# Even mixer: rotated queries and keys turned by way of HBM and VectorE's 32x32 blocks, and one weight remainder computed behind the score maxima

## The chip, the cores and the metric

The kernel runs on one core of one Trainium2 chip. The metric is the device time of one execution in microseconds (us); lower is better.

## What is computed

The program is two transformer blocks in float32 on one sequence of 256 tokens by 1024 features. The first block (two hybrid layers and a norm) is not touched. The second has an even mixer and an odd mixer; the change lies in the even mixer. Cut to what matters:

```python
def even_mixer(h, w_in, pool_w, pool_scale, w_out):
    z = h @ w_in                                   # 256 x 3072, six groups of 512
    q, k, v, ga, pu, gb = split(z)                 # 512 columns each
    q = rope_partial(q.reshape(b, s, 4, 128))      # first 32 of each head's 128 features are rotated
    k = rope_partial(k.reshape(b, s, 4, 128))
    att = moba_attention(q, k, v).reshape(b, s, A) * silu(ga)   # here: causal attention over 256 tokens
    pool = multiscale_pool(pu, pool_w, pool_scale) * silu(gb)   # means over windows of 2, 4, 8, 16 tokens
    return concatenate([att, pool]) @ w_out
```

The scores contract over a head's 128 features, so queries and keys must stand with features on the partitions, while the product h @ w_in of these groups leaves them with tokens on the partitions. Each must be turned.

## The kernel before

The engines are programmed by hand: each block (`sync`, `tensor`, `scalar`, `vector`, `gpsimd`) is a list of instructions in the order in which its engine runs them, and semaphores are the only tie between them. Every matrix product is split into a high and a low part. A weight piece is 128 partitions x 4 x 512 floats (1 MB). SP loads it (L683) into one of four raw slots as soon as VectorE (DVE) has finished with the slot's last piece; ScalarE (ACT) rounds it to `w_hi` (L1518, `split`), DVE computes the remainder `w_lo` = raw - `w_hi` (L1911, `split`), and TensorE (PE) makes three products of them. `step(p)` splits piece p + 2, on ACT as on DVE. `piece_used` counts the pieces that PE is done with; three pieces fit in `w_hi` and `w_lo`.

The even mixer's twelve weight pieces are called E+0 to E+11 here (E is `E_PIECE`). Two pieces make one group of 512 columns: queries (E+0, E+1), keys (E+2, E+3), values (E+4, E+5), the pool input (E+6, E+7), the gate of the pool (E+8, E+9) and the gate of the attention (E+10, E+11). The first three groups come out with tokens on the partitions (`mixer_first`, `tokens_out`), the last three with features on them (`features_out`).

On PE the order is: queries, keys, values; then 16 transposes of 128x128 (L1308) that put queries and keys into four PSUM banks, `TURN`, after `rope2_done` has reached 4; then the pool input; the scores (L1314, L1315), which wait for `q2T_ready` and `k2T_ready`; the gate of the pool; one of four column blocks of the attention's gate, the transposes of the probabilities (L1323) and the pool's product (L1328), which waits for `pool_mean`; and the rest.

ACT evacuates the query and key groups as they are to `zq` and `zk` (`evacuate`, L1530). DVE rotates them there (`rotate_second`, L2289 to L2295). After the transposes ACT copies the turned queries to `q2T` (L1765), DVE the turned keys to `k2T` (L2313). DVE then splits E+9 and E+10, and only then runs through the four heads' scores: scale and mask, two maxima and their negation (L2318 to L2323). ACT's exponentials (L1774) follow each head's maxima, then the Silu table and the gate's evacuation; DVE normalises (L2326, L2329) and splits E+11 and E+12. GpSimd (POOL) computes the window means in `pool_means` (L2572 to L2584) once the pool input has been evacuated and the turned queries and keys have left the area that it writes.

The first block already moves other tensors through HBM: SP stores them to a bounce tensor (`store_rows`, L688) and fetches them back in 32-feature blocks with four DMAs, one per block of partitions (`fetch_blocks`, L694), and DVE turns each 32x32 block in place (`turn_blocks`, L2036). All DMAs are issued by SP, in the order of its list. The names `arena` and `raw` in the profile are areas that many tensors share; `q2T`, `k2T`, `zq`, `zk` and the pool's tensors all read `arena` there.

Of the kernel before, what the change touches and what calls it, by code (L numbers as in the profile page):

```python
# [6 lines left out]
F32 = mybir.dt.float32  # L7
# [5 lines left out]
P = 128  # L13
# [154 lines left out]
def build_program(nc, ins, consts, where, out):  # L168
    ctx = ExitStack()
    with ctx:  # L170
# [147 lines left out]
        q2T = area(11264, ATT2_HEADS, SEQ)  # L318
        k2T = area(12288, ATT2_HEADS, SEQ)
        probs2 = area(13312, ATT2_HEADS, 384)  # L320
        probs2T = area(11264, ATT2_HEADS, 384)
# [143 lines left out]
        rope2_done = sem("rope2_done")  # L465
        qk2_turned = sem("qk2_turned")
        q2T_ready = sem("q2T_ready")
# [170 lines left out]
        def _(sp):  # L638
# [84 lines left out]
            for l in range(DEPTH):  # L723
# [15 lines left out]
                for f in range(-2, F_GROUPS):  # L739
                    if l == DEPTH - 1 and f == 0:  # L740
                        for t in range(T):
                            sp.wait_ge(out_free[t], l * USES + USE_UP)
                        sp.dma_start(g_final, ins["g_final"].partition_broadcast(P)).then_inc(gfinal_landed, 16)
                        sp.dma_start(g_pre[0], ins["pre_norm_g_2"][0].partition_broadcast(P)).then_inc(gpre_landed[0], 16)
                        for b, w in enumerate(("o_b_re_2", "o_b_im_2")):
                            sp.dma_start(b_in[:, b, :, :], ins[w][0].rearrange("(s g) p i -> (g p) s i", g=2)).then_inc(s5_landed, 16)
                        for b, w in enumerate(("o_c_re_2", "o_c_im_2")):
                            sp.dma_start(c_in[:, b, :, :], ins[w][0].rearrange("(j g) o p -> (g o) j p", g=8)).then_inc(s5_landed, 16)
                    if f >= 0:
                        for c in range(2):  # L750
                            rows_f = ins["w_down"][l, f * COLS:(f + 1) * COLS, :]
                            load(square_piece(rows_f, c, 0))
                    if f + 2 < F_GROUPS:
                        for half in range(2):
                            load(square_piece(ins["w_up"][l], f + 2, half))
            for g in range(6):
                for half in range(2):
                    load(square_piece(ins["e_w_in_2"][0], (0, 1, 2, 4, 5, 3)[g], half))
                if g == 1:
                    sp.wait_ge(piece_used, E_PIECE)  # L760
# [39 lines left out]
        def _(pe):  # L800
# [499 lines left out]
            for g in range(1, 3):  # L1300
                tokens_out(E_USE + g, E_PIECE + 2 * g, 2, hT_hi, hT_lo)
            pe.wait_ge(rope2_done, 2 * T)
            for i in range(4):
                for j in (2 * i, 2 * i + 1):
                    for t in range(T):
                        c = (j % 2) * SEQ + t * P
                        src = (zq, zk)[j // ATT2_HEADS][:, t, (j % ATT2_HEADS) * P:(j % ATT2_HEADS + 1) * P]
                        last = pe.transpose(TURN[i][:, c:c + P], src, ident)  # L1308
                last.then_inc(qk2_turned, 1)
            features_out(E_USE + 3, E_PIECE + 6, 2, hT_hi, hT_lo)  # L1310
            pe.wait_ge(q2T_ready, 2)
            pe.wait_ge(k2T_ready, 2)
            for hd in range(ATT2_HEADS):
# [192 lines left out]
        def _(act):  # L1506
# [247 lines left out]
            act.wait_ge(final_scaled, T)  # L1754
            evacuate(E_USE, lambda t: zq[:, t, :])
            step(p + 2)
            step(p + 3)
            evacuate(E_USE + 1, lambda t: zk[:, t, :])
            step(p + 4)
            step(p + 5)  # L1760
            evacuate(E_USE + 2, lambda t: zv[:, t, :])
            step(p + 6)
            for i in range(2):
                act.wait_ge(qk2_turned, i + 1)
                act.activation(q2T[:, 2 * i:2 * i + 2, :].rearrange("p h t -> p (h t)"), TURN[i], copy).then_inc(q2T_ready, 1)  # L1765
            step(p + 7)
# [134 lines left out]
        def _(dve):  # L1901
# [378 lines left out]
            def rotate_second(g, t):  # L2280

                dve.wait_ge(out_free[t], E_USE + g + 1)
                half = ROT2 // 2
                z = (zq, zk)[g][:, t, :].rearrange("p (h d) -> p h d", h=ATT2_HEADS)
                z1, z2 = z[:, :, 0:half], z[:, :, half:ROT2]
# [24 lines left out]
            step(p + 6)  # L2310
            for i in range(2):
                dve.wait_ge(qk2_turned, i + 3)
                dve.tensor_copy(k2T[:, 2 * i:2 * i + 2, :].rearrange("p h t -> p (h t)"), TURN[2 + i]).then_inc(k2T_ready, 1)  # L2313
            step(p + 7)
            step(p + 8)
            for hd in range(ATT2_HEADS):
# [5 lines left out]
                order.link(dve.tensor_reduce(top2[:, hd, 1:2], probs2[:, hd, P:3 * P], AX_X, ALU.max))  # L2322
                dve.tensor_scalar(neg_top2[:, hd, :], top2[:, hd, :], -1.0, None, ALU.mult).then_inc(top2_ready, 1)  # L2323
            for hd in range(ATT2_HEADS):
                dve.wait_ge(exp2_done, hd + 1)
# [209 lines left out]
        def _(pool):  # L2535
# [30 lines left out]
            def pool_means():  # L2566

                pool.wait_ge(pool_zero, 1)
                for b in range(2):
                    pool.wait_ge(out_free[b], E_USE + 4)  # L2570
                pool.wait_ge(qk2_turned, 4)
                order.link(pool.tensor_tensor(pool_s1[:, :, 1:PW], pool_in[:, :, 1:PW], pool_in[:, :, 0:PW - 1], ALU.add))  # L2572
# [160 lines left out]
```

## Time and profile before

| | |
|---|---|
| median of 3 runs | 1009.09 us (1008.75 to 1009.18) |
| profiled execution, its own time | 1008.58 us |
| its span | 1006.8 us |
| mean granted clock of PE | 0.999 |
| busy: PE / DVE / ACT / POOL | 999.8 / 726.5 / 501.8 / 170.3 us |
| instructions | 13509 |
| DMA | 192.80 MB, mean 191 GB/s |

The views used are the page's chain of work that ended last, the waits, the timelines of the engines from 780 to 860 us, the answers for single lines, and a table by stretch. A DMA has two times: what issuing it takes on SP (a timeline's us), and the time from issue to landing. Matmuls are pipelined: the time of one (390 ns for 512 columns) is longer than the distance to the next (0.23 us), and what a group takes is read from starts.

### The profile page before, as it was taken

To read this page: it belongs to the slowest core of one execution; us is meant where nothing else is said; L and a number is where in the kernel's file an instruction comes from. 1 tells how busy PE (TensorE), PEld (TensorE's weight loads), DVE (VectorE), ACT (ScalarE), POOL (GpSimd) and SP (SyncE) were. 2 spreads that over 40 slices of the span, in tenths; PEclk is the share of its full clock that TensorE was granted. 3 is DMA by queue.
4 is the path that set the end of the run, shared out by engine and by line. 5 is a ranking of instruction groups with operands and counts; after the bars stand their busy time and mean duration, and the time that the engine had idled before them with its cause. 6 is when DMAs were issued, how large, how long until landed. Compare 5 with 4: busy or idle time off the path is not lost.

```text
span 1006.8 us, 13509 instructions
## 1 busy us (share of the span) xinstructions
PE 999.8 (99%) x5621; PEld 846.1 (84%) x5621; DVE 726.5 (72%) x805; ACT 501.8 (50%) x610; POOL 170.3 (17%) x129
## 2 busy tenths in 40 slices
PE   9999999999999999999999999999999999999997
PEld 7888787888888888888877888888887899899796
DVE  5885785766665656785785767788877767789974
ACT  6544553455444436444564355444468555644352
POOL 0520000000000000430000020000000149169730
PEclk9999999999999999999999999999999999999999
DMA  9796665555555454597574457556544754355451
GB/s 347 247 297 239 190 187 173 190 182 173 203 186 190 167 195 161 188 297 243 183 218 164 164 165 269 179 177 213 196 167 140 246 168 168 125 168 152 111 188 42
DMA packets 106396, 192.80 MB, mean 191 GB/s; under 512 B 9352, under 2 KB 20704, under 8 KB 106208
## 3 DMA queue, kind: packets, MB, share of 16 engines
q1 hardware_dynamic: 106160, 191.85, 58.1%
q8 instruction: 44, 0.72, 0.3%
q10 hardware_dynamic: 176, 0.09, 0.0%
q14 instruction: 16, 0.13, 0.0%
HBM read 182.79 MB, written 6.82 MB: 188 GB/s over the span
## 4 chain that ended last, share of the span: by engine, by line
PE 99%; DVE 0%; ACT 0%; issue 0%; DVEq 0%; ACTq 0%
PE bank L816 13%; PE bank L818 12%; PE bank L819 12%; PE bank L1121 11%; PE bank L841 10%; PE bank L845 9%; PE bank L852 9%; PE bank L1125 6%; PE bank L1203 2%; PE bank L1430 1%; PE bank L998 1%; PE bank L1014 1%; PE bank L1417 1%; PE bank L850 1%; PE bank L843 1%; PE bank L1106 1%
## 5 line engine op out<-in xcount | busy, mean ns | idle before, releaser
L1911 DVE TENSOR_TENSOR w_lo<-arena,w_hi 128x2048 fp32r<-128x2048 f32 (+1 forms) x80 | 185.0, 2323 | 97.7 <-ACT w_hi L1518 97.3
L1911 DVE TENSOR_TENSOR w_lo<-raw,w_hi 128x2048 fp32r<-128x2048 f32 (+1 forms) x78 | 180.7, 2327 | 80.2 <-ACT w_hi L1518 79.9
L1518 ACT ACTIVATE w_hi<-raw 128x2048 fp32r<-128x2048 f32 (+1 forms) x83 | 157.1, 1893 | 104.9 <-PE bank L819 72.9
L1518 ACT ACTIVATE w_hi<-arena 128x2048 fp32r<-128x2048 f32 (+1 forms) x80 | 151.3, 1892 | 106.0 <-PE bank L819 82.2
L1121 PE MATMUL bank<-hT,w_hi 128*128 128x512 f32 x504 | 123.4, 391 | 0.0
L2539 POOL TENSOR_TENSOR rstd<-mean,const 128x1 f32<-128x1 f32 (+1 forms) x16 | 9.1, 578 | 632.2 <-DVE mean L1920 462.8
L1121 PEld LDWEIGHTS bank<-hT,w_hi 128*128 128x128 f32 x504 | 92.3, 188 | 17.5
L816 PE MATMUL bank<-w_hi,hT 128*128 128x512 f32 (+1 forms) x248 | 95.3, 384 | 0.0
L819 PE MATMUL bank<-w_hi,hT 128*128 128x512 f32 (+1 forms) x224 | 85.5, 382 | 0.0
L818 PE MATMUL bank<-w_lo,hT 128*128 128x512 f32 (+1 forms) x224 | 85.5, 382 | 0.0
L816 PE MATMUL bank<-w_hi,uT_hi 128*128 128x512 f32 x208 | 81.2, 390 | 0.0
L819 PE MATMUL bank<-w_hi,uT_lo 128*128 128x512 f32 x208 | 81.0, 389 | 0.0
L818 PE MATMUL bank<-w_lo,uT_hi 128*128 128x512 f32 x208 | 81.0, 389 | 0.0
L841 PE MATMUL bank<-w_hi,hT 128*128 128x512 f32 (+1 forms) x200 | 77.5, 390 | 0.0
L845 PE MATMUL bank<-w_hi,hT 128*128 128x512 f32 (+1 forms) x200 | 75.8, 381 | 0.0
L1125 PEld LDWEIGHTS bank<-hT,w_lo 128*128 128x128 f32 x504 | 67.1, 191 | 3.9
L841 PE MATMUL bank<-w_hi,uT_hi 128*128 128x512 f32 x176 | 69.3, 394 | 0.0
L845 PE MATMUL bank<-w_hi,uT_lo 128*128 128x512 f32 x176 | 68.8, 391 | 0.0
L1125 PE MATMUL bank<-hT,w_lo 128*128 128x256 f32 x504 | 68.3, 283 | 0.0
L816 PE MATMUL bank<-hT,w_hi 128*128 128x256 f32 x192 | 55.3, 289 | 0.0
L816 PEld LDWEIGHTS bank<-w_hi,hT 128*128 128x128 f32 x248 | 46.6, 188 | 9.1
L818 PE MATMUL bank<-hT,w_hi 128*128 128x256 f32 x184 | 52.1, 283 | 0.0
(356 smaller groups left out, 1915.4 us busy)
## 6 DMA issues: line engine op xcount, KB each, us to landing
arena<-in_w_in SPq DMA_DIRECT2D x22, 1024.0 KB, 5.4
raw<-in_w_in SPq DMA_DIRECT2D x20, 1024.0 KB, 6.0
arena<-in_w_up SPq DMA_DIRECT2D x16, 1024.0 KB, 5.6
raw<-in_w_up SPq DMA_DIRECT2D x16, 1024.0 KB, 5.2
arena<-in_w_down SPq DMA_DIRECT2D x16, 1024.0 KB, 5.1
raw<-in_w_down SPq DMA_DIRECT2D x16, 1024.0 KB, 5.3
raw<-in_e_w_in SPq DMA_DIRECT2D x6, 1024.0 KB, 5.2
arena<-in_e_w_in SPq DMA_DIRECT2D x6, 1024.0 KB, 5.4
```

The source lines that it names most:

```text
L816: pe.matmul(dst, a_hi, b_hi, start=first, stop=False, skip_group_check=shared)
L818: pe.matmul(dst, a_hi, b_lo, start=False, stop=False, skip_group_check=shared)
L819: mm = pe.matmul(dst, a_lo, b_hi, start=False, stop=last_one, skip_group_check=shared)
L841: pe.matmul(dst, a_hi, b_hi, start=(start and i == 0), stop=False, skip_group_check=shared)
L843: pe.matmul(dst, a_hi, b_lo, start=False, stop=False, skip_group_check=shared)
L845: pe.matmul(dst, a_lo, b_hi, start=False, stop=False, skip_group_check=shared)
L852: mm = pe.matmul(dst, a_hi, b_lo, start=False, stop=last_one, skip_group_check=shared)
L1121: pe.matmul(UP[j], w_hi[:, s[i], kk, at[j]], hT[:, k, :, :].rearrange("p e t -> p (e t)"), start=(i == kk == 0), stop=False, skip_group_ch ...
L1125: return pe.matmul(UP[j][:, 0:SEQ], w_lo[:, s[i], kk, at[j]], hT_hi[:, i * KP + kk, :], start=False, stop=(i == 1 and kk == KP - 1), skip_ ...
L1203: last = pe.matmul(OUT[t], a[:, KP * i + k, at[t]], w[:, s[i], k, :], start=(first and k == 0), stop=(last_one and k == KP - 1))
L1518: act.activation(w_hi[:, p % SPLIT_RING, :, 0:n], raw_at(p)[:, :, 0:n], copy).then_inc(hi_ready, 1)
L1911: dve.tensor_tensor(w_lo[:, s, :, 0:n], raw_at(p)[:, :, 0:n], w_hi[:, s, :, 0:n].bitcast(F32), ALU.subtract).then_inc(lo_ready, 1)
```

## The change

Queries and keys are no longer turned on PE:

- ACT's evacuation (`head_blocks`) writes `zq` and `zk` with the columns reordered, 32-feature block first and head second, so that the rotated features of all heads are the first 128 columns; the rotation works on those.
- SP stores each to an HBM bounce (`store_qk2`) and fetches it back in four 32-partition DMAs (`fetch_qk2`), in 512-byte pieces, into `qk2_moved`. The queries' store stands behind the load of E+8; their fetch and the keys' store behind the load of E+10; the keys' fetch behind that of E+11.
- DVE turns the blocks into `q2T` and `k2T`, one instruction each, where it had copied the keys; ACT's two copies and PE's 16 transposes are gone. PE waits for one count of each semaphore ahead of the scores.
- On DVE the split of E+10 (`step(p + 8)`) moves from ahead of the four heads' maxima to behind them.
- POOL's wait for the transposes becomes a wait for both stores.

```diff
+        qk2_moved = [area(17472, T * BLOCKS, ATT2_HEADS * BLOCK), area(18496, T * BLOCKS, ATT2_HEADS * BLOCK)]
+        qk2_bounce = [nc.dram_tensor(f"{w}2_bounce", [T * P, 512], F32, kind="Internal").ap() for w in "qk"]
...
+            def store_qk2(i):
+
+                sp.wait_ge(rope2_done, T * (i + 1))
+                store_rows(qk2_bounce[i].rearrange("(t p) n -> p t n", p=P), (zq, zk)[i], qk2_stored[i])
+
+            def fetch_qk2(i):
+
+                sp.wait_ge(qk2_stored[i], 16)
+                fetch_blocks(qk2_moved[i], qk2_bounce[i], qk2_blocks[i])
+
             for g in range(6):
                 for half in range(2):
                     load(square_piece(ins["e_w_in_2"][0], (0, 1, 2, 4, 5, 3)[g], half))
+                    if (g, half) == (4, 0):
+                        store_qk2(0)
+                    if (g, half) == (5, 0):
+                        fetch_qk2(0)
+                        store_qk2(1)
+                    if (g, half) == (5, 1):
+                        fetch_qk2(1)
...
-            pe.wait_ge(rope2_done, 2 * T)
-            for i in range(4):
-                for j in (2 * i, 2 * i + 1):
-                    for t in range(T):
...
-                        last = pe.transpose(TURN[i][:, c:c + P], src, ident)
-                last.then_inc(qk2_turned, 1)
             features_out(E_USE + 3, E_PIECE + 6, 2, hT_hi, hT_lo)
-            pe.wait_ge(q2T_ready, 2)
-            pe.wait_ge(k2T_ready, 2)
+            pe.wait_ge(q2T_ready, 1)
+            pe.wait_ge(k2T_ready, 1)
...
-            evacuate(E_USE, lambda t: zq[:, t, :])
+            def head_blocks(n, z):
+                for t in range(T):
+                    whole(act, n, t)
+                    act.activation(z[:, t, :].rearrange("p (b h f) -> p h b f", b=BLOCKS, f=BLOCK),
+                                   OUT[t].rearrange("p (h b f) -> p h b f", b=BLOCKS, f=BLOCK), copy).then_inc(out_free[t], 1)
+
+            head_blocks(E_USE, zq)
...
-                act.wait_ge(qk2_turned, i + 1)
-                act.activation(q2T[:, 2 * i:2 * i + 2, :].rearrange("p h t -> p (h t)"), TURN[i], copy).then_inc(q2T_ready, 1)
...
-            for i in range(2):
-                dve.wait_ge(qk2_turned, i + 3)
-                dve.tensor_copy(k2T[:, 2 * i:2 * i + 2, :].rearrange("p h t -> p (h t)"), TURN[2 + i]).then_inc(k2T_ready, 1)
+            for i, (z, done) in enumerate(((q2T, q2T_ready), (k2T, k2T_ready))):
+                dve.wait_ge(qk2_blocks[i], 16 * BLOCKS)
+                turn_blocks(z, qk2_moved[i], ATT2_HEADS).then_inc(done, 1)
             step(p + 7)
-            step(p + 8)
             for hd in range(ATT2_HEADS):
...
                 dve.tensor_scalar(neg_top2[:, hd, :], top2[:, hd, :], -1.0, None, ALU.mult).then_inc(top2_ready, 1)
+            step(p + 8)
...
-                pool.wait_ge(qk2_turned, 4)
+                for i in range(2):
+                    pool.wait_ge(qk2_stored[i], 16)
```

Where this moves instructions, the order on SP shows it first, from the load of E+8 to the first load of the output weights. Before:

```order
L683 DMA raw<-in_e_w_in 128x4x512 x2
L683 DMA arena<-in_e_w_in 128x4x512 x2
L683 DMA raw<-in_e_w_out 128x4x512 x2
```

And after (the numbers of lines have moved; L686 is the load, L691 the store, L697 the fetch):

```order
L686 DMA raw<-in_e_w_in 128x4x512
L691 DMA q_bounce<-arena 128x2x512
L686 DMA raw<-in_e_w_in 128x4x512
L686 DMA arena<-in_e_w_in 128x4x512
L697 DMA arena<-q_bounce 32x8x128 x4
L691 DMA k_bounce<-arena 128x2x512
L686 DMA arena<-in_e_w_in 128x4x512
L697 DMA arena<-k_bounce 32x8x128 x4
L686 DMA raw<-in_e_w_out 128x4x512 x2
```

Ten DMAs stand between the loads, and each holds up those below it while SP waits. On DVE, from the splits of E+7 and E+8 to the first head's maxima, there stood before:

```order
L1911 TENSOR_TENSOR w_lo<-arena,w_hi 128x2048
L1911 TENSOR_TENSOR w_lo<-raw,w_hi 128x2048
L2313 COPY arena<-bank 128x512 x2
L1911 TENSOR_TENSOR w_lo<-raw,w_hi 128x2048
L1911 TENSOR_TENSOR w_lo<-arena,w_hi 128x2048
L2318 SCALAR_TENSOR_TENSOR arena<-bank,const 128x384
L2321 TENSOR_REDUCE top<-arena 128x1
```

And after:

```order
L1926 TENSOR_TENSOR w_lo<-arena,w_hi 128x2048
L1926 TENSOR_TENSOR w_lo<-raw,w_hi 128x2048
L2051 STREAM_TRANSPOSE arena<-arena 128x8x4x32 x2
L1926 TENSOR_TENSOR w_lo<-raw,w_hi 128x2048
L2332 SCALAR_TENSOR_TENSOR arena<-bank,const 128x384
L2335 TENSOR_REDUCE top<-arena 128x1
```

The turns stand where the copies stood, ahead of the split of E+9, and the split of E+10 has left this place; it now follows the fourth head's maxima.

## Rows read from the trace of the kernel before

**Rows 1.** The page's part 4, the chain that ended last, by engine.

```profile
PE 99%; DVE 0%; ACT 0%; issue 0%; DVEq 0%; ACTq 0%
```

**Rows 2.** Waits of PE, whole run: who for whom, us, times, longest.

```profile
PE bank L921 <- DVE h_sb L1945: 1.0, 1, 1.0
PE bank L931 <- DVE hT L1949: 0.2, 1, 0.2
```

**Rows 3.** PE timeline: start us, us, engine, line, operation, out<-in, count.

```profile
804.41 0.39 PE L819 MATMUL bank<-w_hi,hT 128*128 128x512 f32 x1
804.64 1.91 PE L1308 MATMUL bank<-const,arena 128*128 128x128 f32 x16
806.30 0.36 PE L841 MATMUL bank<-hT,w_hi 128*128 128x256 f32 x1
```

**Rows 4.** DVE timeline, the same columns.

```profile
796.39 4.13 DVE L1911 TENSOR_TENSOR w_lo<-arena,w_hi 128x2048 fp32r<-128x2048 f32 x1 [3.47 <-ACT w_hi L1518]
...
802.35 0.22 DVE L2295 TENSOR_TENSOR arena<-arena 128x64 f32<-128x64 f32 x1
...
820.53 2.54 DVE L1911 TENSOR_TENSOR w_lo<-arena,w_hi 128x2048 fp32r<-128x2048 f32 x1 [3.89 <-ACT w_hi L1518]
822.99 0.54 DVE L2318 SCALAR_TENSOR_TENSOR arena<-bank,const 128x384 f32<-128x384 f32 x1
...
828.24 0.17 DVE L2323 TENSOR_SCALAR neg_top<-top 128x2 f32<-128x2 f32 x1
```

**Rows 5.** SP timeline, DMA issues; us is the time issuing takes.

```profile
436.43 1.81 SPq L694 DMA_DIRECT2D arena<-r_bounce  x4
...
800.54 4.80 SPq L683 DMA_DIRECT2D arena<-in_e_w_in  x2
```

**Rows 6.** The line of the weight loads, only the one issued at 800.54.

```profile
DMA to landing us min/median/max: 5.1/5.1/5.1
```

**Rows 7.** The line of all ten stores to HBM bounces.

```profile
DMA to landing us min/median/max: 7.3/7.7/10.2
```

**Rows 8.** The a_bounce fetches issued from 453.4 to 454.7, nothing ahead of them.

```profile
DMA to landing us min/median/max: 2.1/2.2/2.3
```

**Rows 9.** Three stretches: us, DVE busy (count), PE clock, DMA share, GB/s.

```profile
433.00:435.00 2.00, 2.00 (x3) 1.00 1.02 413
438.00:442.00 4.00, 3.96 (x3) 1.00 1.11 208
...
803.00:805.00 2.00, 1.95 (x1) 1.00 1.03 397
```

**Rows 10.** The line of the block turns: ns min/median/max, forms.

```profile
L2036 DVE STREAM_TRANSPOSE arena<-arena x6: 1771/2304/2311, 64.0 to 518.6; 128x2048 f32<-128x2048 f32 x4, 128x1536 f32<-128x1536 f32 x2
```

**Rows 11.** PE timeline, the scores and what follows them.

```profile
817.90 0.39 PE L1314 MATMUL bank<-arena 128*128 128x128 f32 x2
...
826.27 0.28 PE L841 MATMUL bank<-hT,w_hi 128*128 128x256 f32 x1
...
833.47 1.47 PE L1323 MATMUL bank<-const,arena 128*128 128x128 f32 x12
834.78 1.89 PE L1328 MATMUL bank<-pool_m,pool_w 128*128 128x256 f32 x8
```

**Rows 12.** POOL timeline, the window means.

```profile
818.92 1.99 POOL L2572 TENSOR_TENSOR arena<-arena 128x1084 f32<-128x1084 f32 x1 [20.55 <-ACT arena L1530]
821.00 3.46 POOL L2573 TENSOR_TENSOR arena<-arena 128x807 f32<-128x807 f32 x1
...
830.93 2.44 POOL L2584 TENSOR_TENSOR pool_m<-pool_m,arena 128x1024 f32<-128x1024 f32 x1
```

**Rows 13.** ACT timeline; in brackets the idle time before and its releaser.

```profile
793.95 0.60 ACT L1530 ACTIVATE arena<-bank 128x512 f32<-128x512 f32 x1 [2.12 <-PE bank L819]
...
812.40 1.91 ACT L1518 ACTIVATE w_hi<-raw 128x2048 fp32r<-128x2048 f32 x1 [4.19 <-PE bank L819]
...
831.33 1.91 ACT L1518 ACTIVATE w_hi<-arena 128x2048 fp32r<-128x2048 f32 x1
```

More of the change, by code:

```diff
@@ L465, in build_program @@
         rope2_done = sem("rope2_done")
-        qk2_turned = sem("qk2_turned")
+        qk2_stored = [sem(f"{w}2_stored") for w in "qk"]
+        qk2_blocks = [sem(f"{w}2_blocks") for w in "qk"]
         q2T_ready = sem("q2T_ready")
@@ L1301, in _ @@
                 tokens_out(E_USE + g, E_PIECE + 2 * g, 2, hT_hi, hT_lo)
-            pe.wait_ge(rope2_done, 2 * T)
-            for i in range(4):
-                for j in (2 * i, 2 * i + 1):
-                    for t in range(T):
-                        c = (j % 2) * SEQ + t * P
-                        src = (zq, zk)[j // ATT2_HEADS][:, t, (j % ATT2_HEADS) * P:(j % ATT2_HEADS + 1) * P]
-                        last = pe.transpose(TURN[i][:, c:c + P], src, ident)
-                last.then_inc(qk2_turned, 1)
             features_out(E_USE + 3, E_PIECE + 6, 2, hT_hi, hT_lo)
-            pe.wait_ge(q2T_ready, 2)
-            pe.wait_ge(k2T_ready, 2)
+            pe.wait_ge(q2T_ready, 1)
+            pe.wait_ge(k2T_ready, 1)
             for hd in range(ATT2_HEADS):
@@ L1754, in _ @@
             act.wait_ge(final_scaled, T)
-            evacuate(E_USE, lambda t: zq[:, t, :])
+            def head_blocks(n, z):
[4 more added lines that the diff above has]
+            head_blocks(E_USE, zq)
             step(p + 2)
             step(p + 3)
-            evacuate(E_USE + 1, lambda t: zk[:, t, :])
+            head_blocks(E_USE + 1, zk)
             step(p + 4)
@@ L2283, in rotate_second @@
                 half = ROT2 // 2
-                z = (zq, zk)[g][:, t, :].rearrange("p (h d) -> p h d", h=ATT2_HEADS)
+                z = (zq, zk)[g][:, t, 0:ATT2_HEADS * BLOCK].rearrange("p (h d) -> p h d", h=ATT2_HEADS)
                 z1, z2 = z[:, :, 0:half], z[:, :, half:ROT2]
@@ L2310, in _ @@
             step(p + 6)
-            for i in range(2):
-                dve.wait_ge(qk2_turned, i + 3)
-                dve.tensor_copy(k2T[:, 2 * i:2 * i + 2, :].rearrange("p h t -> p (h t)"), TURN[2 + i]).then_inc(k2T_ready, 1)
+            for i, (z, done) in enumerate(((q2T, q2T_ready), (k2T, k2T_ready))):
+                dve.wait_ge(qk2_blocks[i], 16 * BLOCKS)
+                turn_blocks(z, qk2_moved[i], ATT2_HEADS).then_inc(done, 1)
             step(p + 7)
-            step(p + 8)
             for hd in range(ATT2_HEADS):
```

## The prediction

> **What bounds the kernel now.** I read the chain that ended last first: PE holds 99% of it [rows 1]. The waits of PE say how complete that is: in the whole run it waited twice, 1.0 and 0.2 us, both at the very start [rows 2]. So from the first matmul on, one PE instruction starts when the one before it lets it, in the even mixer too. Two things follow. Work taken off PE shortens the run by its whole length, if nothing that PE waits for then comes too late; and work put on another engine costs nothing as long as it is ready before PE asks. The prediction is therefore one subtraction and a list of deadlines, each of which moves earlier with PE.
>
> **Off PE: the 16 transposes.** They start at 804.64, and the first matmul of the pool input at 806.30 [rows 3]: 1.66 us, 0.104 each. The matmul ahead of them starts at 804.41, 0.23 before, which is the usual distance of matmuls of 512 columns, so the pool input can start at 804.64 and nothing of the 1.66 is pipeline that stays. Bounds: 1.6 to 1.8 (the first matmul behind the transposes takes 0.36 where its kind takes 0.28 [rows 3, 11], and that may go too). All deadlines below are the old ones less 1.66. Two copies on ACT and two on DVE go as well; on PE's chain they are worth nothing.
>
> **The deadline of the turned keys.** The scores started at 817.90 [rows 11]; PE will ask at 817.90 - 1.66 = 816.24. The queries are stored long before, and fetched behind the load of E+10; the keys are the ones that can be late. Their way, step by step:
>
> The second half of the keys is rotated at 802.35 + 0.22 = 802.57 [rows 4]. It was that late because the split of E+6 ahead of it took 4.13 us. SP issues the load of E+10 at 800.54 and, until 800.91, does nothing else [rows 5]; then the four fetches of the queries, 1.81 us as four of their kind took in the first block [rows 5]: 802.72. So the keys' store is issued at about 802.75, hardly behind the rotation.
>
> When it lands I get from two sides. By the stores that the trace shows, 7.3 to 10.2 us after issue [rows 7]: 810.1 to 813. By bytes in the queue, which move in the order of issue: the load of E+10 lands 5.1 after its issue [rows 6], 805.7; the queries are 0.52 MB in 512-byte pieces; fetches of 1-KB pieces moved 208 GB/s with the DMA engines full, loads 397 and stores of 4-KB rows 413 [rows 9]. With 208 that is 2.5 us, 808.2; the keys' store of 0.52 MB 1.3 us more, 809.5. The stores of the rows are mostly larger or behind more bytes, so I take the lower of these, between 809.5 and 810.1.
>
> SP then issues the keys' four fetches; it is held there while the load of E+11, issued at 800.54 + 4.80 - 0.37 = 804.97 [rows 5], is already in the queue: its 1.05 MB at 397 GB/s are 2.6 us, 812.1. The keys' 0.52 MB follow at 208 GB/s: 814.6. The floor is that of issuing: the last fetch issued at 809.5 + 1.4 = 810.9 cannot land before 813.0, since a fetch in an empty queue took 2.1 to 2.3 [rows 8]. DVE's turn of 128x1024: 2304 ns for 2048 and 1771 for 1536 [rows 10], 1.04 ns an element, so 1.24 us with the wake-up 1.35: **ready at 816.0**, 0.2 before PE asks. With the store at 810.1 it is 0.4 later, a wait of 0.4. I take the middle, a wait of 0.2 us. The ends: ready at 814.4 (no wait, 1.9 to spare), and with a store of 10.2 us ready at about 818.9 (813 + 1.4 + 3.2 for data and landing + 1.35), a wait of 2.7.
>
> The rule that the Trainium skill has for such pieces is kinder: "DMA: Bandwidth & Descriptors", section Specifications, says that pieces of 512 B and more move at line rate, 435 GB/s. The 1-KB fetches of this trace moved 208 with full engines [rows 9], so the trace does not agree. By the page's figure an estimate is 1.2 us for each fetch, the keys some 2.6 us earlier and no wait at all; by the row it is the sum above.
>
> **What DVE does with the turns.** Two turns are 2.5 us where two copies stood. The queries' turn falls between the splits of E+8 and E+9 where DVE was idle. The keys' turn, ending at 816.0, does delay the split of E+9, whose `w_hi` was ready at 812.40 + 1.91 [rows 13], 812.65 now: it runs from 816.0 to 818.3. PE needs that remainder in the gate's second piece, from 826.27 - 1.66 = 824.6 on [rows 11]: 6 us to spare, no cost. ACT's evacuations, 0.60 each [rows 13], now write in another order, for which no row exists: I bound them by 0.60 and 1.20. The keys' second one is issued at 793.95, and the rotation could not start before the split of E+6 ended at 800.52 [rows 4, 13], so this costs nothing either.
>
> **The moved remainder.** Before, the split of E+10 held the maxima until 822.99, and they ended at 828.24 + 0.17 [rows 4], 5.4 us later. Now they run from 818.3 to 823.7, the split behind them to 826.0; PE wants it at 833.47 - 1.66 - 0.7 = 831.1 [rows 11]. The normalised probabilities come at 827 to 830, where PE's transposes start at 833.47 - 1.66 = 831.8 [rows 11]. Left as it was, this would have been the next late thing; moved, it has 2 us. Its own worth on the chain is nothing, it only keeps the deadline.
>
> **Sum.** 1008.58 - 1.66 + 0.2 = 1007.1 for a profiled run; the median of before stands 0.5 above its profiled run, so 1007.6, which is 0.15% faster. A difference under about 0.2% (2.0 us) is not told from none here, so even the whole gain of 1.66 counts as no change.
>
> **Rival 1: POOL's window means become late.** PE asked for them at 834.78 [rows 11], now 833.1. Their chain took 818.92 to 830.93 + 2.44 [rows 12]. Within it the instruction at 821.00 took 3.46 us for 807 elements, where 1084 took 1.99: 2.0 us of it is waiting while DVE's split, begun at 820.53, ran to 823.07 [rows 4, 12]. So the two exclude each other, and who starts first finishes first. Now the chain could start at 817.26; the split of E+9 until 818.3 puts it 1.0 later, the split of E+10 falls into it as before, and its last instruction would start at 830.93 - 1.66 + 1.0 = 830.3. But ACT, which before reached the split of E+11 only at 831.33 [rows 13] behind exponentials and table load, is now early: the first half of the gate is complete half a group's piece (2.9 us) after 824.6, so `w_hi` of E+11 is there at 827.5 + 0.8 + 1.9 = 830.2, and DVE starts its split then. If DVE wins this race by a tenth, POOL starts at 832.5 and ends at 834.4: PE waits 1.2 us. Time: 1007.6 + 1.2 = 1008.8. If the keys are ready before 814.9, POOL wins clearly; if they are late, DVE does. The rule stands in "SBUF — State Buffer" of the Trainium skill, section SBUF: two separate sides: a DVE operation with two SBUF inputs and a GpSimd one that reads SBUF hold the shared port exclusively, first come first served; the trace agrees, by the 2.0 us above.
>
> **Rival 2, slower: small pieces cost by the piece.** If the DMA engines pass 512-byte pieces no faster than 1-KB ones (208 GB/s is 0.2 pieces a ns), each fetch of 1024 pieces takes 5.0 us instead of 2.5. That delays the queries' fetch, the keys' store behind it and the keys' own fetch: 816.0 + 5.0 = 821.0 ready, a wait of 4.8. Time: 1009.1 - 1.7 + 4.8 = 1012.2. It decides from a fetch of about 3.4 us on, where the wait eats the 1.66 gained; past 0.2% slower from 4.4. Against it: 1-KB pieces may be bound by bytes into 32 partitions rather than by count, which the row can't tell.
>
> **Rival 3: the keys are late by a store like the slowest shown.** 0.6 to 2.7 us of wait: 1008 to 1010.1.
>
> **Rival 4: it does not do what it says.** Were the transposes hidden in PE's pipeline, nothing would be gained: 1009.1 or more. The starts in [rows 3] speak against it.
>
> **How the numbers follow.** Forecast (gain kept but for a wait of 0 to 0.6, 1007.1 to 1008.0): 0.42. Rival 1: 0.26. Rival 3: 0.12. Rival 2: 0.12. Rival 4 0.03, and 0.05 for a gain larger than PE's part. Time 1007.6. The range goes from 1006.8 (1.8 gained, no wait, and 0.5 us of scatter) to 1010.3 (rival 3's end), and leaves out rival 2 and little else. Faster by over 0.2%, below 1007.07: the larger gain and the lucky edge of the forecast, 0.12. Slower by over 0.2%, above 1011.1: rival 2 and a little, 0.12. Within: 0.76.
>
> **What would show it.** In the profile after: the pool input starts at 804.64; the first score 1.66 earlier, or later with a DMA or DVE named as its releaser among PE's waits; the keys' store landing 7 us after issue and their last fetch near 814.6; the turn 1.24 us; the split of E+9 right behind the keys' turn; POOL's last instruction against DVE's split of E+11, and PE's pool product with or without a wait. The prediction is wrong if PE's stream elsewhere does not slide by the same 1.66, if the fetches take 5 us, or if a second deadline in the odd mixer, where DVE is busy almost throughout, proves tied to something that has not moved.

## The result and the profile after

The changed kernel took 1013.36 us (median of 6 runs, 1011.28 to 1014.95), beside 1009.05 (1008.75 to 1009.5) for the kernel before: 1.0039 times as long, interval [1.0028, 1.005]. That is 4.3 us slower, where 1007.6 was forecast, and outside the range that was given (1006.8 to 1010.3). Two more measurements of the same kernel, below, gave 2.8 and 2.5 us slower. The profiled run took 1014.95 us, its span 1013.2, against 1008.58 and 1006.8.

In the page's part 4, the chain that ended last, PE no longer holds 99% [rows 1]:

```profile
PE 94%; DMA 3%; DVE 1%; SPq 1%; ACT 1%; issue 0%; DVEq 0%; ACTq 0%
```

A DMA is on the chain. PE's waits in the whole run (who for whom, us, times, longest) name the place, beside those of [rows 2]:

```profile
PE bank L1326 <- DVE arena L2051: 3.6, 1, 3.6
PE bank L941 <- DVE h_sb L1960: 1.0, 1, 1.0
PE bank L861 <- ACT arena L1542: 0.7, 1, 0.7
```

L1326 is the first score, L2051 the turn on DVE (the 0.7 is in another block, ahead of 703 us). The PE timeline, at the end of the values' use and at the scores, the places of [rows 3] and [rows 11]:

```profile
806.11 0.39 PE L839 MATMUL bank<-w_hi,hT 128*128 128x512 f32 x1
806.33 0.28 PE L861 MATMUL bank<-hT,w_hi 128*128 128x256 f32 x1
...
817.73 0.28 PE L839 MATMUL bank<-hT,w_lo 128*128 128x256 f32 x1
821.60 0.77 PE L1326 MATMUL bank<-arena 128*128 128x128 f32 x2 [3.59 <-DVE arena L2051]
822.16 1.06 PE L1327 MATMUL bank<-arena 128*128 128x256 f32 x2
```

The transposes are gone, and the pool input starts 0.22 behind the last product, as forecast. That it starts at 806.33 and not at 804.64 has another reason: the whole stream was already 1.7 us late in this run, and had been since 62 us. The scores ask at 817.85 and get the keys at 821.60. And they run slower than in [rows 11]: a group of 256 columns takes 1.06 where it took 0.60. The table by stretch (us, PE, weight loads, DVE, ACT, POOL busy, granted clock, DMA share, GB/s) shows why:

```profile
817.90:821.60 3.70, 0.11 (x2) 0.04 (x1) 1.40 (x2) 2.40 (x2) 2.67 (x2) 0.89 0.33 111
821.60:827.40 5.80, 5.80 (x19) 5.08 (x20) 5.70 (x8) 0.98 (x4) 5.56 (x5) 0.50 0.24 72
828.00:832.00 4.00, 4.00 (x36) 4.00 (x35) 3.86 (x9) 3.34 (x13) 3.83 (x6) 1.00 0.29 107
```

For 5.8 us behind the wait the granted clock is 0.50, the lower of the two levels (1.2 GHz), and then 1.00 again. The trace's clock records put the half clock from 820.76 to 827.59.

What came late was the keys. SP's timeline (the us are those of issuing), and under it what the DMA view gives for stretches that hold a single issue each: the load of E+10, that of E+11, the keys' store, the first and the last of the keys' fetches; the last figure is the time to landing:

```profile
802.66 2.15 SPq L697 DMA_DIRECT2D arena<-q_bounce  x4
804.85 0.45 SPq L691 DMA_DIRECT2D k_bounce<-arena  x1
806.68 0.39 SPq L686 DMA_DIRECT2D arena<-in_e_w_in  x1
811.57 1.80 SPq L697 DMA_DIRECT2D arena<-k_bounce  x4
```

```profile
arena<-in_e_w_in SPq DMA_DIRECT2D x1, 1024.0 KB, 5.5
arena<-in_e_w_in SPq DMA_DIRECT2D x1, 1024.0 KB, 10.9
k_bounce<-arena SPq DMA_DIRECT2D x1, 512.0 KB, 6.7
arena<-k_bounce SPq DMA_DIRECT2D x1, 128.0 KB, 3.4
arena<-k_bounce SPq DMA_DIRECT2D x1, 128.0 KB, 7.3
```

The first three fetches land 3.4 to 4.1 us after issue, the fourth 7.3. The load of E+11 takes 10.9, where in the kernel before the same load (issued at 804.98) landed in 5.7; here the queries' fetches and the keys' store, 1 MB together, are ahead of it. DVE's timeline closes the chain:

```profile
811.17 1.24 DVE L2051 STREAM_TRANSPOSE arena<-arena 128x1024 f32<-128x1024 f32 x1
820.21 1.25 DVE L2051 STREAM_TRANSPOSE arena<-arena 128x1024 f32<-128x1024 f32 x1 [7.79 <-DMA arena<-k_bounce]
821.37 3.23 DVE L1926 TENSOR_TENSOR w_lo<-raw,w_hi 128x2048 fp32r<-128x2048 f32 x1
```

**A ledger.** PE holds the chain but for this wait, so one instruction's start in this trace, less the start of the same one in the trace of before, says how much was lost or won up to there. The four points are the products that in the kernel before start at 702.6, 806.5, 857.4 and 1000.5 us, and each column is the change between two of them (later is +):

| profiled run | up to 702.6 | to 806.5: the transposes | to 857.4: wait, half clock | to 1000.5 | all |
|---|---|---|---|---|---|
| the change | +1.71 | -1.77 | +6.73 | -0.25 | +6.42 |
| after_again | +0.12 | -1.71 | +5.35 | -0.23 | +3.53 |
| after_third | +0.39 | -1.72 | +4.58 | -0.14 | +3.11 |
| load_after_store | +0.57 | -1.76 | +6.29 | -0.25 | +4.85 |
| filled_wait | +1.02 | -1.76 | +3.78 | -0.25 | +2.79 |
| hold_next_load | +0.49 | -1.77 | +4.37 | -0.25 | +2.84 |
| fetch_first | +0.66 | -1.74 | +0.01 | +0.06 | -1.01 |
| no_key_trip | +0.64 | -1.71 | 0.00 | -0.25 | -1.32 |
| early_keys | +1.09 | -1.72 | 0.00 | -0.25 | -0.88 |

The third column can be put together again. In the change PE stood from 817.85 (one distance of 0.12 behind the last product) to 821.60, 3.75; behind it 6.0 us at half clock lose 3.0: 6.75, and the ledger has 6.73. After_again: 3.62 + 3.41 / 2 = 5.33, ledger 5.35. After_third, where 3.16 of the half clock's 3.41 us fall behind the wait: 2.96 + 3.16 / 2 = 4.54, ledger 4.58.

### The profile page after: what moved, and what is told of

Same layout as the page of the kernel before. It is cut to its first block, busy times and chain, and to the rows that moved or that the text cites. A ratio compares the mean times of both kernels' runs of the same rounds, so it can differ in the third digit from the quotient of the medians.

```text
span 1013.2 us, 13485 instructions
## 1 busy us (share of the span) xinstructions
PE 1001.5 (99%) x5605; PEld 846.4 (84%) x5605; DVE 727.7 (72%) x805; ACT 501.0 (49%) x608; POOL 170.0 (17%) x129
## 4 chain that ended last, share of the span: by engine, by line
PE 94%; DMA 3%; DVE 1%; SPq 1%; ACT 1%; issue 0%; DVEq 0%; ACTq 0%
PE bank L836 13%; PE bank L838 12%; PE bank L839 12%; PE bank L1141 11%; PE bank L861 9%; PE bank L865 8%; PE bank L872 8%; PE bank L1145 6%; PE bank L1223 2%; DMA raw<-in_w_in 2%; PE bank L1442 1%; PE bank L1034 1%; PE bank L1429 1%; DMA arena<-k_bounce 1%; DMA k_bounce<-arena 1%; PE bank L1126 1%
```

## The experiments

Each run stands beside the kernel before on the same chip, which took 1009.2 to 1009.4.

**after_again**, the changed kernel as it is.

> The changed kernel once more, on the chip of the next three. Theory A (the keys come back late: PE waits about 3.6 us for them and then runs some 6 to 7 us at the lower clock, which costs about 3 more): 1011.5 to 1014, the wait and the half clock in its profile again, the wait's length moving from run to run with the landing of the keys' last fetch. Theory B (the changed program starts worse: in the profile after, PE's stream is 1.7 us behind before's from the 34th us on): the same 1.7 us at the start again, in every run. If the shift at the start is chance, it is gone or differs here.

Measured: 1012.07 us (1009.8 to 1013.61), ratio 1.0026 [1.0015, 1.0037]. The stream is 0.1 late at 702.6 and not 1.7, so that share of the first profile was scatter of the start-up. The wait and the half clock are there again. PE's wait, and the stretch at half clock:

```profile
PE bank L1326 <- DVE arena L2051: 3.5, 1, 3.5
```

```profile
820.00:823.00 3.00, 3.00 (x10) 2.64 (x11) 3.00 (x2) 0.00 (x0) 2.92 (x2) 0.50 0.01 4
```

The fetches land 3.9, 4.2, 4.5 and 7.1 us after issue, the load of E+11 10.7.

**remainder_only**, the kernel before with nothing but the moved split:

```diff
             step(p + 7)
-            step(p + 8)
             for hd in range(ATT2_HEADS):
...
                 dve.tensor_scalar(neg_top2[:, hd, :], top2[:, hd, :], -1.0, None, ALU.mult).then_inc(top2_ready, 1)
+            step(p + 8)
```

> The kernel before with nothing changed but the split of E+10 moved behind the maxima. Theory A: within 0.2 us of before, 1009.1, since PE waits for nothing there. Rival C (the moved remainder or its contention with POOL costs part of the 4.3 us): 1010 or more, with a wait of PE for the window means or for the probabilities.

Measured: 1009.46 (1009.0 to 1012.94), ratio 1.0006 [0.9997, 1.0015]; no wait of PE that the kernel before did not have. The move costs nothing.

**no_key_trip**, the changed kernel without the keys' store and fetch (both turns read the queries' blocks, so the scores are of queries with queries):

```diff
                     if (g, half) == (5, 0):
                         fetch_qk2(0)
-                        store_qk2(1)
-                    if (g, half) == (5, 1):
-                        fetch_qk2(1)
...
-                dve.wait_ge(qk2_blocks[i], 16 * BLOCKS)
-                turn_blocks(z, qk2_moved[i], ATT2_HEADS).then_inc(done, 1)
+                dve.wait_ge(qk2_blocks[0], 16 * BLOCKS)
+                turn_blocks(z, qk2_moved[0], ATT2_HEADS).then_inc(done, 1)
...
-                for i in range(2):
-                    pool.wait_ge(qk2_stored[i], 16)
+                pool.wait_ge(qk2_stored[0], 16)
+                pool.wait_ge(rope2_done, 2 * T)
```

> The changed kernel with the keys' store and fetch left out; both turns read the queries' blocks, so the scores are those of queries with queries. All else as changed. Theory A: no wait and no lower clock, the whole 1.66 us of the transposes gained, 1007.4. Theory B: the shift at the start stays, 1009.1. Rival C: still above 1009.

Measured: 1007.4 (1007.1 to 1008.44), ratio 0.9982 [0.9973, 0.9991]. No wait at the scores, no half clock, and 1.9 us less than before. Everything that the change loses hangs on the keys' trip; the queries' trip, the turns, ACT's new order and POOL cost nothing by themselves.

**early_keys**, the keys one piece earlier: rotated ahead of the split of E+6, stored ahead of the load of E+10, fetched right behind it and ahead of the load of E+11. POOL, which writes another table ahead of the means, waits for that rotation.

```diff
-                    if (g, half) == (5, 0):
+                    if (g, half) == (4, 1):
                         fetch_qk2(0)
                         store_qk2(1)
-                    if (g, half) == (5, 1):
+                    if (g, half) == (5, 0):
                         fetch_qk2(1)
...
             step(p + 3)
-            step(p + 4)
             for t in range(T):
                 rotate_second(1, t)
+            step(p + 4)
...
-            pool.wait_ge(out_free[1], E_USE + 2)
+            pool.wait_ge(rope2_done, 2 * T)
```

> The changed kernel with the keys' trip begun earlier: they are rotated ahead of the split of E+6, stored ahead of the load of E+10 and fetched right behind it, and POOL's tap table waits for that rotation. Theory A: keys turned by about 812, 4 us ahead of the scores; no wait, no lower clock, 1007.4. Theory B: 1009.1. Rival D (the extra 2 MB on the queue are what costs, whenever they move): above 1009.5.

Measured: 1007.01 (1006.76 to 1007.68, 10 runs), ratio 0.9976 [0.9967, 0.9986]: the best of all, 2.3 us below before. SP's timeline has the store and the fetches 7 and 8 us ahead of those above:

```profile
797.73 0.45 SPq L691 DMA_DIRECT2D k_bounce<-arena  x1
802.83 0.39 SPq L686 DMA_DIRECT2D arena<-in_e_w_in  x1
803.26 2.13 SPq L697 DMA_DIRECT2D arena<-k_bounce  x4
```

DVE starts the two turns at 810.60, one behind the other; PE takes the first score at 817.27, without a wait. These fetches too stand right behind a load, and land 5.8, 5.8, 6.0 and 6.0 us after issue, none behind the others.

After these four the keys were the cause, and the question was why their last fetch lands 3 us behind the third.

**hold_next_load.** Theory E: the load of E+12, issued right behind the fetches, takes the DMA engines from them. So it is held back until they have landed.

```diff
                     if (g, half) == (5, 1):
                         fetch_qk2(1)
+                        sp.wait_ge(qk2_blocks[1], 16 * BLOCKS)
```

> The changed kernel, but SP waits until the keys' four fetches have landed before it issues the load of E+12. In the two profiles of the changed kernel the first three of these fetches landed 3.4 to 4.5 us after issue, the last 7.1 and 7.3. Theory E (the last fetch is late because its pieces share the engines with the load issued right behind it): the last lands like the others, near 4.5, the keys are turned 2.7 us earlier, PE waits about 1 us, 1008.5 to 1009. Rival F (what is queued ahead, the load of E+11 and the store, makes it late): the last fetch still takes 7 us and PE waits 3.5 us or more, 1012.

Measured: 1010.67 (1009.2 to 1012.11), ratio 1.0015 [1.0005, 1.0024]; a wait of 2.5 us. The fetches still land spread, 3.5, 3.9, 4.1 and 6.0 us after issue, with nothing behind them. So what is behind them is not the main cause: at most it counts for about 1 us of the last one's 7.1, and even that is not sure, since in the other profiles of kernels with this order of DMAs the last one takes 6.3 to 7.4.

**fetch_first.** Theory F: it is what stands ahead in the queue. The fetches go ahead of the load of E+11; they can't be issued much earlier for it, since SP waits for the store.

```diff
                         fetch_qk2(0)
                         store_qk2(1)
-                    if (g, half) == (5, 1):
                         fetch_qk2(1)
```

> The changed kernel, but the keys' fetch stands ahead of the load of E+11 on SP instead of behind it; rotation and store stay where they are. Theory F (bytes ahead of the fetch): the fetch moves behind the store alone, lands near 813, the keys are turned by 814.5, no wait and no lower clock: 1007.5. Theory E (the load right behind it shares the engines): the last fetch still lands 7 us after issue, near 817, and PE waits about 2 us: 1010.5.

Measured: 1007.54 (1007.05 to 1008.25), ratio 0.9981 [0.9971, 0.9991]. The SP and DVE timelines:

```profile
803.90 0.45 SPq L691 DMA_DIRECT2D k_bounce<-arena  x1
810.78 1.80 SPq L697 DMA_DIRECT2D arena<-k_bounce  x4
```

```profile
815.21 1.25 DVE L2050 STREAM_TRANSPOSE arena<-arena 128x1024 f32<-128x1024 f32 x1 [3.83 <-DMA arena<-k_bounce]
```

Issued from 810.78 to 812.1, the fetches land in 2.4, 2.8, 2.9 and 3.1 us; the turn starts at 815.21, and PE does not wait. After_again issues them 0.8 earlier, behind the load, and turns at 818.54. F is right, and E is not: the load of E+11 now stands right behind the fetches.

**scores_1_later, scores_2_later.** The change as it is, but PE takes the scores behind one or two column blocks of the gate's piece, `features_out(E_USE + 4)`, instead of ahead of it: a later deadline for the same keys. The diff is that of the first; the second has `(0, 1)` for `(0, 0)`.

```diff
+            def scores2():
+
+                pe.wait_ge(q2T_ready, 1)
...
-            features_out(E_USE + 4, E_PIECE + 8, 2, hT_hi, hT_lo)
+            features_out(E_USE + 4, E_PIECE + 8, 2, hT_hi, hT_lo, after={(0, 0): scores2})
```

> The changed kernel with the scores placed on PE behind the first of the eight column blocks of the pool's gate (12 matmuls, 1.44 us), the keys' trip as it is. Theory A, which counts a wait of 3.8 us and behind it a stretch at the lower clock: the wait shrinks to 2.4 us; if the clock falls as before, 1010.5, if it does not, 1010. Rival: if something other than the keys holds PE, the time stays at 1012.

> The same with the scores behind two column blocks (24 matmuls, 2.9 us). Theory A: a wait of 0.9 us, too short for the clock to fall if its fall goes with the length of the wait: 1008.5. If the clock falls all the same, 1009.5 or more. The probabilities come 1 us later than their place before; if they become the next thing that PE waits for, a new wait stands ahead of their transposes.

Measured: 1010.87 (1008.53 to 1012.28), ratio 1.0009 [0.9999, 1.0018], and 1010.01 (1008.51 to 1010.81), ratio 1.0005 [0.9996, 1.0014]. With one block the wait shrinks to 2.1 us, half clock behind it (3.41 us); with two it is gone in the profiled run, and the next late thing shows, the probabilities, whose transposes L1338 has:

```profile
PE bank L1338 <- DVE arena L2347: 1.0, 1, 1.0
```

That wait of 1.0 us was followed by no half clock. This profile is of the fastest of the ten runs (1008.51, as expected); the median is 1.5 us above it, and what the slower runs lose is open. The deadline can't be moved far: the next thing behind the scores becomes late.

**after_third** is the change again, beside the next three.

> The changed kernel once more, as the companion of the other three of this group. By the earlier runs 1012 to 1013.5, a wait of 3.5 us for the turned keys, the four landings of their fetch at about 3.5, 4, 4.5 and 7 us, and a half clock of 3.4 or 6.8 us behind the wait.

Measured: 1011.69 (1009.55 to 1012.85), ratio 1.0022 [1.0012, 1.0032]; a wait of 2.8 us, the half clock 3.41 us, the last fetch 6.6 us after issue.

**filled_wait.** Is the half clock an answer to PE's standing still? PE does ten products that nobody needs (queries with queries, into the banks of the scores) where it would wait for the keys:

```diff
             pe.wait_ge(q2T_ready, 1)
+            for i in range(5):
+                pe.matmul(TURN[i % 4][:, 0:P], q2T[:, i % 4, 0:P], q2T[:, i % 4, 0:P], start=True, stop=True)
+                pe.matmul(TURN[i % 4][:, P:3 * P], q2T[:, i % 4, P:SEQ], q2T[:, i % 4, :], start=True, stop=True)
             pe.wait_ge(k2T_ready, 1)
```

> The changed kernel, with ten extra products put in the place where TensorE waits for the turned keys, behind the wait for the queries: five times (128 and 256 columns, f32), 0.64 us each at full clock, 3.2 us in all, of the queries with themselves, into the banks that the scores overwrite. The scores and all behind them are as in the change. Theory G (the half clock that followed the wait is an answer to TensorE's standing still, and costs 1.7 to 3 us beside the wait): the rest of the wait is under 1 us, the granted clock stays at 1.00 behind it, and the median comes 1.5 us or more below that of the change, at 1010.0 to 1010.6. Rival: the half clock has another cause, or was no cost; then the extra products change nothing, 1011.6 to 1012.5.

Measured: 1010.93 (nine of ten runs 1010.26 to 1011.32; the tenth took 1674.94 and is left out), ratio 1.0015 [1.0005, 1.0024]. Two stretches, the added products and what comes behind them:

```profile
817.20:820.20 3.00, 3.00 (x21) 2.79 (x20) 0.67 (x1) 2.40 (x2) 1.99 (x1) 1.00 0.48 159
821.00:826.00 5.00, 5.00 (x37) 4.79 (x38) 4.93 (x6) 0.26 (x1) 4.76 (x4) 1.00 0.16 27
```

The keys came as late as ever (last fetch 7.4 us after issue), a wait of 0.2 was left, and the granted clock stayed at 1.00. So the half clock is the answer to standing still. The gain on after_third is 0.8 us in the medians, half of the 1.6 that its half clock cost by the ledger. The two profiled runs show why: up to 857.4 this kernel loses 3.78 us and after_third 4.58. The 1.6 of the clock are saved, and 0.8 of them are lost again since the keys came that much later in this run (last fetch 7.4 us after issue, not 6.6). In runs whose keys come sooner the filling costs its 3.2 us all the same (after_third has one at 1009.55, this kernel none under 1010.26); that it lifts the median is likely and not tested. The mechanism holds; both sizes that I had expected (1010.0 to 1010.6, and 1.5 us or more below the change) were missed.

**load_after_store.** Fetch_first leaves open whether any load just ahead spreads the fetches (theory J), or whether a DMA engine has fallen behind while the queue never ran empty (theory H). Here the load of E+11 waits for the keys' store to land, so the queue empties, and the fetches stand behind it as in the change.

```diff
                     if (g, half) == (5, 0):
                         fetch_qk2(0)
                         store_qk2(1)
+                        sp.wait_ge(qk2_stored[1], 16)
```

> The changed kernel, except that the load of E+11 is issued only when the keys' store has landed, so the queue is empty when it starts; the keys' fetches still stand behind that load. Theory H (some DMA engine has fallen behind the others while the queue was never empty, and its share of the keys comes last): with the queue emptied the four fetches land within 1 us of one another, the last at 5 us or less after issue; the load lands 5 us after its issue as in the kernel before, the keys are turned at about 817.5, the wait is 1 to 2 us and the median 1009 to 1010.5. Theory J (any load just ahead of the fetches spreads them): the last lands 2.5 us or more behind the third, 7 us after issue, and the median is 1011 to 1013.

Measured: 1012.08 (1010.65 to 1013.38), ratio 1.0028 [1.0016, 1.004]. The queue was empty from 810 to 811. The stretch, then load, second and last fetch:

```profile
810.00:811.00 1.00, 1.00 (x11) 1.00 (x10) 1.00 (x2) 0.00 (x0) 0.00 (x0) 1.00 0.00 0
```

```profile
arena<-in_e_w_in SPq DMA_DIRECT2D x1, 1024.0 KB, 5.6
arena<-k_bounce SPq DMA_DIRECT2D x1, 128.0 KB, 6.0
arena<-k_bounce SPq DMA_DIRECT2D x1, 128.0 KB, 5.9
```

The load lands in 5.6 us again instead of 10.2 to 10.9, and all four fetches take 5.9 to 6.1: the last is no longer behind the others by more than its issue. H fits the spread, and J does not; the fetches of early_keys, right behind a load and not spread, say the same. The times that I wrote under H were wrong: 5 us for the last fetch and 1009 to 1010.5 left out that the load now starts 5 us later, with all of its 2.6 us ahead of the keys. The turn started at 818.77, no sooner than in after_again, and PE waited 3.3 us.

**early_old_remainder**, early_keys with the split of E+10 back ahead of the maxima.

> The version with the keys a piece earlier (1007.0), with the split of E+10 back ahead of the maxima as in the kernel before. By the prediction's reckoning the maxima then end at about 828.2, the normalised probabilities at 831 to 832.5, where TensorE's transposes start at 831.8: a wait of 0 to 1 us that names VectorE as releaser, 1007.0 to 1008.0. Rival: the moved remainder is worth nothing here either, no wait, 1007.0 within 0.4.

Measured: 1007.3 (1006.8 to 1007.74), ratio 0.9981 [0.9972, 0.9991]; no wait of PE at the probabilities. Against early_keys' 1007.01 that is 0.3 us, which these runs can't tell from nothing. The moved remainder wasn't needed.

## Why the prediction was wrong

**Off PE: 1.66 us.** Right. All profiled runs without the transposes win 1.7 to 1.8 between 702.6 and 806.5, inside the bounds given, 1.6 to 1.8. A further 0.25 is won behind 857 in most of them and in some not; I have no cause for it. Without the keys' trip the time is 1007.4, where 1007.6 was forecast with a wait of 0.2.

**The keys' way up to the store.** Right. The rotation waited for the split of E+6, the four fetches of the queries took 2.15 us to issue and not 1.81, in the runs with the changed kernel's order the store went out at 803.38 to 804.85 and landed 6.5 to 6.9 us later; forecast were 802.75 and 6.75 to 7.35. In after_again it landed by 810.0.

**The step that failed** is the next: "The keys' 0.52 MB follow at 208 GB/s: 814.6." The time of the data was not far off. In fetch_first, with no load ahead, the first fetch went out at 810.78 and the last had landed at 812.1 + 3.1 = 815.2, 4.4 us in all. What was wrong is to take the queue for one pipe, in which a DMA lands when the bytes ahead of it and its own have gone through. In after_again the fourth fetch, issued at 811.4, landed at 818.5: 3.9 us behind the forecast, of which 0.5 is the later issue, 2.7 is its lag behind the third (7.1 after issue against 4.5), and the small rest the data. So the keys were ready at 819.9 and not at 816.0. The landing waits for the slowest of the DMA engines' shares. In the trace of the changed kernel the packets of 512 bytes that start from 816.38 on are 64 of the 1024, one sixteenth: they leave one after the other until 819.3, and the other 960 had started by 816.1. The Trainium skill describes this counting in "DMA: Bandwidth & Descriptors", section Why a DMA increments its semaphore by 16 and not by 1: a DMA runs on up to 16 engines that finish independently, and its semaphore is full only with the last of them. The trace agrees, by the 3.2 us between the times to landing of the third fetch and the fourth.

I had the warning in my rows. Loads land 5.1 us after issue in [rows 6], but in a queue that runs empty between two of them. The same stretch of both kernels, 803 to 818, before and after:

```profile
803.00:818.00 15.00, 15.00 (x121) 14.64 (x121) 7.74 (x5) 5.88 (x6) 0.00 (x0) 1.00 0.61 197
...
803.00:818.00 15.00, 15.00 (x112) 14.22 (x110) 6.89 (x11) 5.58 (x6) 0.00 (x0) 1.00 1.03 289
```

The DMA share was 0.61 and became 1.03. With pauses a share that is behind can catch up, without them it can stay behind; so I read these two lines. Why one falls behind by 3 us is open. A packet of 16 KB of instructions passes in each of these traces, about 1.05 us long, and may hold up one engine. In the seven with the changed order of DMAs up to the keys' fetches it starts at 809.4 to 810.9, in the full queue, a little before the keys' fetches. In fetch_first (810.2) and load_after_store (809.8) it passes just as the queue runs empty. So no run tells this packet apart from the full queue as such, and it is the rival that stands.

**The end of the range.** It took a store of 10.2 us as the worst case (ready at 818.9, a wait of 2.7). The store was never the trouble; the fetch was, with about 3 us, and nothing in the list of rivals had a late share of a DMA.

**A term that was missing** is what a wait costs beyond its length. I priced every wait, in rival 3 up to 2.7 us, at its length alone. In the profiled runs waits of 2.1 to 3.6 us were each followed by half clock, four times for 3.41 us and twice for 6.83: 1.6 to 3.0 us more. Waits of 1.0 us (scores_2_later) and 0.2 (filled_wait) were followed by none. With it, rival 3's 2.7 becomes 4.4 (with the shorter half clock, 1.7) and the range ends at 1012.0 instead of 1010.3. That takes in one of the three measurements of this kernel (1011.69), misses one by 0.1 (1012.07), and the first, 1013.36, clearly. In after_again the two together make the miss: a wait of 0.2 was forecast, and 3.6 of standing and 1.7 of clock were lost. The Trainium skill, in "TensorE: Matmul & The Clock Gate", section Terms, puts the penalty at the throttled time by the share of pulses left out, half of it; the ledger agrees within 0.05 us in three runs.

**Rival 1**, POOL's means, did not occur, but by little. In the changed kernel the late keys put the race off: POOL's last instruction started at 832.79 and took 2.51, DVE's split of E+11 started only at 838.46, and PE's product with the means at 841.45. The race as forecast was run in fetch_first, where the keys are in time. POOL's last instruction, and DVE's split of E+11:

```profile
830.62 2.40 POOL L2599 TENSOR_TENSOR pool_m<-pool_m,arena 128x1024 f32<-128x1024 f32 x1
```

```profile
830.70 4.47 DVE L1925 TENSOR_TENSOR w_lo<-arena,w_hi 128x2048 fp32r<-128x2048 f32 x1 [0.74 <-ACT w_hi L1529]
```

POOL won by 0.08 us, and the split, 2.28 alone, had to wait for it. The means were ready at 833.02, PE's product with them started at 833.70. The forecast had POOL at 830.3 and the split at 830.2, and this trace is 0.66 late, so both times were right to about 0.3 us and the order was luck. What losing the race would have cost was counted too low: the 1.2 us leave 1.9 for POOL's last instruction, and [rows 12] has 2.44, which makes it 1.8. No run shows it.

**Rival 2** gave 1012.2, which is near the result, by a mechanism that was absent. Pieces of 512 bytes are not slower by the piece: at 0.2 pieces a ns they would move 102 GB/s, and the table of stretches for fetch_first has 245 while they move. Judged by the time alone, the wrong cause would have been credited.

```profile
812.00:814.00 2.00, 2.00 (x19) 2.00 (x18) 0.00 (x0) 1.23 (x1) 0.00 (x0) 1.00 1.02 245
```

**Rival 3**, late keys, was the right one in kind, with 0.12; its cause, a slow store, was not, and its price lacked the clock. That the keys were late all the same is luck for this rival.

**The remainder and the turns.** The turns took 1.24 and 1.25 us as computed. The split of E+9 behind the keys' turn took 3.23 in the first profile beside POOL and cost nothing. That the remainder "would have been the next late thing" was wrong by early_old_remainder: there the split of E+10 waits until 819.25 for ACT's `w_hi`, which would hold for keys at 816.0 as well.

## What to carry to other kernels

When a transpose is sent through memory, put the fetch ahead of the next bulk load and not behind it, or begin the trip a piece earlier: the last of the same four fetches landed in 3.1 us ahead of a load and in 7.1 behind it, and the kernel took 1007.5 or 1012.1; with the earlier trip it took 1007.0. To let the queue run empty first and keep the load ahead (load_after_store, 1012.1) gained nothing. A deadline that a chain of DMAs meets by 0.2 us on paper should be priced by the slowest share of a DMA, not by bytes alone. And a wait of 2 us or more on an engine that was busy all along is priced at its length and at the slower clock that followed it in every such run here.

## What the runs showed of the hardware that I had not expected

- In a queue that did not run empty for 15 us, a load of 1 MB took 10.2 to 10.9 us to land. Bytes ahead are part of it: behind the queries' fetches alone (no_key_trip) it took 7.1, and in the kernel before 5.7. The last of four small fetches behind it took 1.9 to 3.2 us longer than the third; one engine's share was that far behind.
- Waits of PE of 2.1 to 3.6 us were each followed by half clock, waits of 1.0 and 0.2 by none. The half clock did not begin with the wait: it began between 1.1 us before PE went on (load_after_store, 0.8 in the change) and 1.0 us after (hold_next_load), and stayed for 3.41 or 6.83 us though PE was then busy.
- DVE and POOL took turns within a tenth of a microsecond: the split that was ready 0.08 us behind POOL's start took 4.47 us instead of 2.28.
- The whole stream of PE starts 0.1 to 1.7 us later from run to run, already at 62 us. In a profiled run that is as large as the effect looked for; the place of a loss is found only by comparing starts along the stream.
